# Mixture-of-experts stage: token rows gathered as 128 halves of 2 KB instead of 64 rows of 4 KB

## What is computed

```python
def hier_moe(x, g_ffn, w_group, w_router, w_gate, w_up, w_down):
    h = rmsnorm(x, g_ffn).reshape(b * t, d)                  # d = 1024
    ...                                                      # best of 4 groups, then the best 2 of its 8 experts
    def add_expert(acc, params):
        wg, wu, wd, c = params                               # 1024x512, 1024x512, 512x1024 each
        act = jax.nn.silu(h @ wg) * (h @ wu)
        return acc + (act @ wd) * c[:, None], None
    out, _ = lax.scan(add_expert, jnp.zeros_like(h), (w_gate, w_up, w_down, combine))   # 32 experts
```

## Time and profile before

| | |
|---|---|
| median of 3 runs | 1159.38 us (1159.24 to 1162.21) |
| profiled execution | 1159.31 us, its span 1157.5 us |
| TensorE | 1026.8 us busy, 89% of the span |
| VectorE, ScalarE, GpSimd | 433.2, 243.2, 298.5 us |
| DMA | 304.27 MB, mean 263 GB/s; from slice 25 on about 400 |

### The profile page before, as it was taken

How to read it: one execution, slowest core, us unless ns; L and a number is a source line. 1 busy time by engine, 2 the same in 40 slices (tenths; PEclk the granted TensorE clock), 3 DMA queues, 4 the chain that set the end, 5 groups by cost and what they waited for, 6 DMA issues and landing times. The chain is left out here.

```text
span 1157.5 us, 16104 instructions
## 1 busy us (share of the span) xinstructions
PE 1026.8 (89%) x5989; PEld 574.5 (50%) x5989; DVE 433.2 (37%) x1203; ACT 243.2 (21%) x550; POOL 298.5 (26%) x262
## 2 busy tenths in 40 slices
PE   6999999998999999989999499998777778877786
PEld 3644444446777775323565355454434445444443
DVE  3655888886557555222344211111111111011122
ACT  2122321113444554210043111111110110111011
POOL 1033414533544433002000123222312222221211
PEclk9999999999999999999999699999999999999999
DMA  6331132236756346797482889999999999999993
GB/s 204 93 105 41 52 111 100 83 112 208 230 156 216 112 142 248 256 369 232 192 344 111 331 345 401 401 389 388 403 404 403 400 398 409 402 406 402 405 398 113
DMA packets 82465, 304.27 MB, mean 263 GB/s; under 512 B 23138, under 2 KB 27362, under 8 KB 70226
## 3 DMA queue, kind: packets, MB, share of 16 engines
q1 hardware_dynamic: 64658, 273.47, 61.9%
q0 software_dynamic: 9824, 16.98, 5.2%
q10 hardware_dynamic: 7904, 12.78, 3.0%
HBM read 290.09 MB, written 29.72 MB: 276 GB/s over the span
## 5 line engine op out<-in xcount | busy, mean ns | idle before, releaser
L403 PE MATMUL p_z<-k_w,k_xT 128*128 128x512 f32 (+2 forms) x528 | 208.1, 548 | 0.0
L403 PEld LDWEIGHTS p_z<-k_w,k_xT 128*128 128x128 f32 (+1 forms) x528 | 92.0, 188 | 102.1 <-issue 100.9
L871 PE MATMUL a_G<-k_xT,k_w 128*128 128x260 f32 x512 | 127.6, 394 | 0.0
L2036 DVE TENSOR_TENSOR e_hid<-e_hid,e_G 128x256 f32<-128x256 f32 x32 | 13.5, 421 | 262.4 <-ACT e_hid L1949 262.4
L1954 ACT ACTIVATE e_y<-e_Y,x_share 64x512 f32<-64x512 f32 x64 | 43.7, 683 | 319.7 <-PE e_Y L1839 310.8
L871 PEld LDWEIGHTS a_G<-k_xT,k_w 128*128 128x128 f32 x512 | 93.3, 192 | 26.5 <-issue 13.6
L966 POOL TENSOR_TENSOR k_x<-k_x 128x512 f32<-128x512 f32 x64 | 80.5, 1271 | 89.6 <-DVE k_side L1032 67.2
L2077 POOL DMA_INDIRECT out_y_p<-e_y,x_table x32 | 45.0, 1408 | 215.8 <-ACT e_y L1954 133.3
L156 POOL DMA_INDIRECT k_rows<-token_rows,x_table x32 | 31.3, 978 | 165.9 <-PE e_TX L1819 154.0
L2041 DVE TENSOR_TENSOR e_hid<-e_hid,e_U 128x256 f32<-128x256 f32 x32 | 13.5, 421 | 133.6 <-PE e_U L1825 133.6
L1242 PE MATMUL g_ring<-k_oT,k_w 128*128 128x512 f32 x128 | 60.1, 616 | 0.0
(11 more groups left out here) (354 smaller groups left out, 1468.0 us busy)
## 6 DMA issues: line engine op xcount, KB each, us to landing
k_w<-in_w_in SPq DMA_DIRECT2D x11, 2048.0 KB, 8.2
k_xT<-in_w_down SPq DMA_DIRECT2D x11, 2048.0 KB, 45.2
x_page<-in_w_down SPq DMA_DIRECT2D x10, 2048.0 KB, 44.1
x_w_out<-in_w_down SPq DMA_DIRECT2D x10, 2048.0 KB, 44.5
k_w<-in_w_gate SPq DMA_DIRECT2D x8, 2048.0 KB, 41.9
k_w<-in_w_up SPq DMA_DIRECT2D x8, 2048.0 KB, 45.1
k_oT<-in_w_gate SPq DMA_DIRECT2D x8, 2048.0 KB, 44.3
k_side<-in_w_up SPq DMA_DIRECT2D x8, 2048.0 KB, 44.7
```

The source lines that it names most:

```text
L403: last = nc.tensor.matmul(z[u % 3][0:p, 0:WIDTH[k]], s.xT[:, j, 128 * i:128 * i + p], s.w[:, c % 2, j, 0:WIDTH[k]], start=j == 0, stop=j = ...
L871: last = nc.tensor.matmul(G[u % 2][:, 0:HT], s.w[:, q % 2, j, 128 * c:128 * c + 128], s.xT[:, j, HT * h:HT * h + HT], start=j == 0, stop=j ...
```

## The change

Each token row is gathered as two halves of 512 numbers. Place q's first half lands in partition q, its second in partition 64 + q, so a gather fills 128 partitions with 2 KB each. It has 128 indices (`s.halves`: twice the row number, plus one in the upper 64 partitions). Four transposes of 128 by 128 turn them, and VectorE's copy takes the two halves of each as separate blocks. To have the table in all 128 partitions, `place` now writes both halves of `Rk` at once, and two operations on VectorE make `s.halves` before `s.table`. The output adds still use `s.table` with 64 places.

```diff
+    c[:, C_HALF] = (p >= CAP) - 2.0
...
-    nc.gpsimd.indirect_dma_start(out=s.xg[n], out_offset=None, in_=s.rows[:, :],
+    nc.gpsimd.indirect_dma_start(out=s.xg[n], out_offset=None, in_=s.half_rows[:, :],
                                  in_offset=bass.IndirectOffsetOnAxis(ap=rows, axis=0),
-                                 bounds_check=TOK - 1, oob_is_err=False).then_inc(s.xg_in[n], 16)
+                                 bounds_check=2 * TOK - 1, oob_is_err=False).then_inc(s.xg_in[n], 16)
...
             def place(i):
-                v.tensor_tensor(Rk[0:p, :, 0, :], bcast(iota(CAP)[0:p], 2, 1), bcast(rank, CAP, 2), ALU.is_equal)
+                v.tensor_tensor(Rk[0:p], bcast(bcast(iota(CAP)[0:p], 2, 1), 2, 1), bcast(bcast(rank, 2, 2), CAP, 3), ALU.is_equal)
...
             def share(i):
-                v.tensor_tensor(Rk[0:p, :, 1, :], bcast(iota(CAP)[0:p], 2, 1), bcast(rank, CAP, 2), ALU.is_equal)
...
             dve.wait_ge(tabled, TILES)
-            link(v.tensor_scalar(unfilled, TBt[0:CAP, :], 0.0, NO_ROW, ALU.is_equal, ALU.mult))
-            v.scalar_tensor_tensor(s.table[:, 0:NE], TBt[0:CAP, :], -1.0, unfilled, ALU.add, ALU.add).then_inc(table_ready, 1)
+            v.tensor_scalar(unfilled, TBt, 0.0, NO_ROW, ALU.is_equal, ALU.mult)
+            link(v.tensor_scalar(twice, TBt, 2.0, s.c[:, C_HALF:C_HALF + 1], ALU.mult, ALU.add))
+            v.tensor_tensor(s.halves[:, 0:NE], twice, unfilled, ALU.add).then_inc(table_ready, 1)
+            v.scalar_tensor_tensor(s.table[:, 0:NE], TBt[0:CAP, :], -1.0, unfilled[0:CAP, :], ALU.add, ALU.add)
...
-        TX, AT = ps("TX", [128, KD, CAP]), s.bankO[:, 0:256].rearrange("p (f t) -> p f t", f=2)
+        TX, AT = ps("TX", [128, 4, 2 * CAP]), s.bankO[:, 0:256].rearrange("p (f t) -> p f t", f=2)
...
         def turn_rows(j):
-            for b in range(KD):
-                last = nc.tensor.transpose(TX[:, b, :], xg[j][:, 128 * b:128 * b + 128], s.ident[0:CAP, 0:CAP])
+            for c in range(4):
+                last = nc.tensor.transpose(TX[:, c, :], xg[j][:, 128 * c:128 * c + 128], s.ident[:])
             return last
...
+            def turned_into(j):
+                return v.tensor_tensor(xT[:, j].rearrange("p (h c) q -> p h c q", h=2), TX[:].rearrange("p c (h q) -> p h c q", h=2),
+                                       bcast(s.gffn[:].rearrange("p (h c) -> p h c", h=2), CAP, 3), ALU.mult)
...
             for n in range(2):
-                gather_rows(nc, s, n, s.table[:, n:n + 1])
+                gather_rows(nc, s, n, s.halves[:, n:n + 1])
...
-                    gather_rows(nc, s, e % 2, s.table[:, e + 2:e + 3])
+                    gather_rows(nc, s, e % 2, s.halves[:, e + 2:e + 3])
...
+    s.half_rows = s.rows.rearrange("t (h d) -> (t h) d", h=2)
...
+        s.halves = sb("halves", [128, NBLK], I32)
...
-        s.xg = [s.rowbuf[0:CAP, 2 * n + 2:2 * n + 4, :].rearrange("p a w -> p (a w)") for n in range(2)]
+        s.xg = [s.rowbuf[:, n + 2, :] for n in range(2)]
```

More of the change, by code:

```diff
@@ L45 @@
 C_E, C_ET, C_HM, C_IOTA, C_TOK, C_THR, C_MH, C_PAR = 896, 960, 968, 976, 1040, 1045, 1061, 1069
-C_DH, C_DB, C_SB, C_END = 1070, 1074, 1082, 1086
+C_DH, C_DB, C_SB, C_HALF, C_END = 1070, 1074, 1082, 1086, 1087
 def constants():
@@ L67, in constants @@
     c[:, C_DB:C_SB] = (p[:, None] % 32 // 4) == np.arange(8)
-    c[:, C_SB:C_END] = (p[:, None] % 32 // 8) == np.arange(4)
+    c[:, C_SB:C_HALF] = (p[:, None] % 32 // 8) == np.arange(4)
+    c[:, C_HALF] = (p >= CAP) - 2.0
     return c
@@ L1152, in merge @@
         Lm, Lm2, C = (small[:, 40 + 32 * n:72 + 32 * n] for n in range(3))
-        unfilled, early = small[0:CAP, 232:232 + NE], small[0:CAP, 264:264 + NE]
+        unfilled, early, twice = small[:, 232:232 + NE], small[0:CAP, 264:264 + NE], small[:, 392:392 + NE]
         prank = small[:, 296:296 + 2 * NE].rearrange("p (k e) -> p k e", k=2)
@@ L1780, in experts @@
         sem = lambda n: ctx.enter_context(nc.semaphore("e_" + n))
-        idx = sb("idx", [CAP, 2], I32)
+        idx = sb("idx", [128, 3], I32)
         xg = s.xg
@@ L1795, in experts @@
         eid = spare[:, 180:180 + NX + 1]
-        unfilled, early = spare[0:CAP, 200:200 + NX], spare[0:CAP, 216:216 + NX]
+        unfilled, early, twice = spare[:, 200:200 + NX], spare[0:CAP, 216:216 + NX], spare[:, 232:232 + NX]
         cmp = spare[:, 256:256 + NE * NX].rearrange("p (a b) -> p a b", a=NE)
@@ L1977, in spread @@
                     dve.wait_ge(u_done, e - 1)
-                v.tensor_tensor(xT[:, e % 2], TX[:], bcast(s.gffn[:], CAP, 2), ALU.mult).then_inc(xT_out, 1)
+                turned_into(e % 2).then_inc(xT_out, 1)
             link = Chain(dve, extra_chain)
@@ L2025, in tables_out @@
                 dve.wait_ge(extra_tabled, 1)
-                link(v.tensor_scalar(unfilled, TB[0:CAP, 0:NX], 0.0, NO_ROW, ALU.is_equal, ALU.mult))
-                link(v.scalar_tensor_tensor(s.table[:, NE:NBLK], TB[0:CAP, 0:NX], -1.0, unfilled, ALU.add, ALU.add))
+                link(v.tensor_scalar(unfilled, TB[:, 0:NX], 0.0, NO_ROW, ALU.is_equal, ALU.mult))
+                link(v.tensor_scalar(twice, TB[:, 0:NX], 2.0, s.c[:, C_HALF:C_HALF + 1], ALU.mult, ALU.add))
+                link(v.tensor_tensor(s.halves[:, NE:NBLK], twice, unfilled, ALU.add))
+                link(v.scalar_tensor_tensor(s.table[:, NE:NBLK], TB[0:CAP, 0:NX], -1.0, unfilled[0:CAP, :], ALU.add, ALU.add))
                 link(v.tensor_scalar(early, TB[0:CAP, 0:NX], 1.0 + SEQ, NO_ROW, ALU.is_lt, ALU.mult))
@@ L2057, in step @@
                 dve.wait_ge(x_turned, b + NE + 1)
-                v.tensor_tensor(xT[:, 0], TX[:], bcast(s.gffn[:], CAP, 2), ALU.mult).then_inc(xT_out, 1)
+                turned_into(0).then_inc(xT_out, 1)
                 dve.wait_ge(gated, b + NE + 1)
@@ L2099, in step @@
                 pool.wait_ge(x_turned, b + NE)
-                nc.gpsimd.tensor_copy(idx[:, 0:1], s.table[:, bass.ds(b + NE, 1)]).then_inc(idx_ready, 1)
-                nc.gpsimd.tensor_copy(idx[:, 1:2], s.to_s[:, bass.ds(b + NE, 1)]).then_inc(idx_ready, 1)
-                pool.wait_ge(idx_ready, b * 3 + 2)
+                nc.gpsimd.tensor_copy(idx[:, 0:1], s.halves[:, bass.ds(b + NE, 1)]).then_inc(idx_ready, 1)
+                nc.gpsimd.tensor_copy(idx[0:CAP, 1:2], s.table[:, bass.ds(b + NE, 1)]).then_inc(idx_ready, 1)
+                nc.gpsimd.tensor_copy(idx[0:CAP, 2:3], s.to_s[:, bass.ds(b + NE, 1)]).then_inc(idx_ready, 1)
+                pool.wait_ge(idx_ready, b * 4 + 3)
                 pool.sem_inc(idx_ready, 1)
@@ L2106, in step @@
                 pool.sem_inc(y_passed, 1)
-                add_rows(0, idx[:, 0:1], idx[:, 1:2])
+                add_rows(0, idx[0:CAP, 1:2], idx[0:CAP, 2:3])
                 pool.wait_ge(y_added, b * 32 + NE * 32 + 32)
```

## The result

The changed kernel takes **1139.27 us** (median of 4, 1138.33 to 1140.74) against 1159.31 (median of 4, 1157.98 to 1162.21) before, a ratio of 0.9822 with an interval of 0.9802 to 0.9842. It is faster by 20 us, 1.8%.

A forecast was written before the change was run, and what follows sets the result against it. Weight bytes through the DMA queues were taken to bound the expert stage. From 1159.31 us, relief -15.6, more packets +1.9 and the head +2.9 gave -10.8, so 1148.5 us; range 1143 to 1165, own range 1143 to 1153.

The forecast's parts named there:

- What bounds the kernel: Expert stage, about 670 to 1141 us: weight bytes through the DMA queues set the time, slowed while gathered rows arrive.
- Relief, -15.6: Weight stream: gathers into 128 partitions take the slump away for 29 gathers, 15.6 us saved.
- The price of 0.54 us a gather: Weight stream, 830 to 1130 us: slow weight packets cost 9.1 us over 17 gathers, 0.54 us each.
- More packets, +1.9: Weight stream: 128 halves instead of 64 rows per gather make more packets, 1.9 us added.
- The head, +2.9: Before expert 0: VectorE's added work and a longer first gather delay the stream by 2.9 us, bounds 0.3 and 4.
- The four more turns beside the weight queue: First gather: 8 pieces per engine instead of 4, alternating with weight packets, 2.4 us added, bounds 0 and 2.6.
- VectorE's operations: Head: wider placing of tile 3 and added operations before the stage's last copy, 0.3 us added.
- Turns, nothing: TensorE's transposes of gathered rows: four of 128 columns instead of eight of 64, no change in time.
- The third, shared turns: Rival: added pieces share turns, so the head costs 0.5 us instead of 2.9, total 1146.1 us; chance 0.06.
- The first, half relief: Rival: engines' pieces go to partitions other engines feed, so collisions spread; -7.8 us relief, total 1156.3 us; chance 0.24.
- The second, no relief: Rival: the burst of 32 scattered rows causes the slump, so weights stay slow; total 1164.1 us; chance 0.24.
- The explanation by ports: Gathers in the stream: partitions 0 to 63 reach only 8 of 16 SBUF ports, hence the slump; no separate size.

The follow-up runs named there:

- mirrored against mirrored: Places 32 to 63 of each expert filled from the far end, in the kernel before (1153.92 us) and in the changed kernel (1134.96 us).
- the mirrored kernel: The changed kernel with places 32 to 63 of each expert filled from the far end: 1134.96 us.
- the long list: The kernel before, same 4 KB rows in partitions 0 to 63, with an index list of 128 places, the upper 64 out of bounds: 1154.46 us.
- the two gathers of halves apart: The kernel before with 2 KB halves by two gathers of 64 places, into partitions 0 to 63 and 64 to 127: 1161.14 us.
- the spread: The changed kernel with an expert's filled places spread over the list, rank 8j + g at place 8g + j: 1158.89 us.

## Why the prediction was right or wrong

**What bounds the kernel: right.** The weights' bytes set the time, the slump behind each gather was the loss, and it went where the prediction had placed it: 16.04 us per expert (16.1 forecast), 432 GB/s in the stretch where rows arrive, 26.6 KB per us in the weight queue. What it didn't see is that the engines' unequal loads are a second cost, the same before and after the change (44.8 and 44.2 us on the first engine, by the count above).

**Relief, -15.6: too small.** The last landing came 20.7 us earlier, and the head gave 1.2 of these, so the stream gave 19.5; with even loads, mirrored against mirrored, it is 19.0. The price of 0.54 us a gather for the slow weights was nearly right. From 690 to 1100 us, with 27 gathers, the weight queue moved 25.5 KB per us before and 26.6 after:

```profile
q1 hardware_dynamic: 12487, 156.69, 93.5%
...
q1 hardware_dynamic: 12963, 163.34, 93.6%
```

That is 15.2 us, 0.56 for each, or 16.3 for 29. What the sum left out is the rest. The gathered packets are faster too: for the gathers of experts 15 to 29 queue 0 spent 189 ns a row before and 161 after, which over the 952 rows of 29 gathers is 1.6 us. The prediction had put up to 3.8 us for this into the range, from 225 ns a row in one stretch of 3 us. And in the last 16 us before the landing the engines idled 4.4 us before and 3.0 after, which gives another 1.4. With these the stream comes to 19.3.

**More packets, +1.9: nothing.** The prediction took it that each half is a packet of its own; the counts are equal.

**The head, +2.9: it was -1.2.** The four more turns beside the weight queue rest on the same error and don't exist: the first gather took 8.14 us, not 11 or more. VectorE's operations cost about what was forecast, 0.2 us for 0.3: from the first line of the placing to the last copy it takes 5.53 us instead of 5.32. The profiled execution hides it, since its placing began 0.25 us earlier and the last copy so came at 650.33 instead of 650.37.

```profile
644.80 0.23 DVE L1672 TENSOR_TENSOR g_scp<-g_ring,x_oh 128x64 f32<-128x64 f32 x1 [0.29 <-PE g_ring L1332]
...
650.33 0.19 DVE L1773 COPY x_share<-x_O 128x32 f32<-128x32 f32 x1 [1.13 <-PE x_O L1351]
```

GpSimd holds a gather of 128 places for 1.05 us instead of 0.98, 0.07 where 0.2 had been put. Expert 0's up product starts at 667.28 where it was 668.47, and so the next weight loads go out 1.2 us sooner. One execution of each stands behind this: the mirrored kernel, whose head is the same, started that product at 668.22, so the size of the head's gain is not sure.

**Turns, nothing: right.** Four transposes take 0.59 us instead of 0.64, beside the loads.

The stream's 19.5 and the head's 1.2, less 0.8 us more behind the last landing (17.8 instead of 16.9), are the 19.9 by which the two profiled executions differ; the 19.5 is what this leaves to the stream. So the steps that failed are the added packets and their turns, priced at 1.9 and 2.4 us and nothing in the runs, and the relief, 3.9 too small. Even with every term at its most favourable bound the sum gives 1140.8; no bound allowed that the added pieces make no packets, or that the head gets shorter.

**The rivals.** The third, shared turns, was what happened, and had 0.06; the page of the Trainium skill that it names fits, and I read 41 packets beside 41 in the earlier trace rows as 41 turns without asking what one record holds. But taking out the turns alone gives 1146.1. Of the 6.7 us from there to the measured time the relief has 3.9, the packets 1.9 and the head 1.7, against 0.8 at the end. The first, half relief, had the idea that the explanation below needs, in the wrong kernel: pieces that go to partitions other engines feed. It was asked of the change; by the mapping it holds for the kernel before. The second, no relief, is refuted: by it the burst of scattered rows itself slows the weights, and in the changed kernel the same burst does not.

**The explanation by ports: only half right.** The prediction followed the Trainium skill, "SBUF — State Buffer", section "Door 1: The DMA port swizzle": 64 partitions, 8 of 16 ports. But the long list writes all its rows through the same 8 ports, and its weights are not slowed; the two gathers of halves apart use all 16 ports and slow them. What is shown is the condition: one transfer that reaches over all 128 partitions keeps the rate (four kernels of two lengths of list and two sizes of piece), transfers over 64 lose it. What may lie behind it is who writes through a port. A weight load covers 128 partitions, and by the page's mapping engine 0 alone writes 0 to 3 and 32 to 35; a gather over all 128 would keep to that. A gather over 64 would send two engines to each of the lower ports, and only engine 0 would meet its own. The Trainium skill, "DMA: Bandwidth & Descriptors", section "Back-pressure in remote DMA", says of transfers between cores that a stalled write stalls the engine's other queues too. If that holds here as well, the weights of an engine wait behind a row that meets a busy port. The slump agrees with it, but no run here looks inside an engine, so this last step is argued, not shown. The page's mapping of a transfer to 128 partitions, taken for the gather, would have spoken against the first rival before the change.

## What to carry to other kernels

Beside a full stream of weights, let one transfer of the gather reach over all 128 partitions, as the stream's do, with 128 places or with every other partition; two transfers of 64 neighbouring partitions do not do it. It is not the pieces' size that counts. Then count the rows by engine: where places are filled from the front, some engines always have more, and a fixed permutation of the places can be worth several us or cost 20. When a queue shows the full rate and its last transfer is late, look at the DMA share in the last us before it lands: 0.5 or 0.25 there says what part of the engines everything waits for.

## What was not expected of the hardware

- The same 1040 rows and the same 128 partitions cost 22 us more in two gathers of 64 places than in one of 128 (1161.14 against 1139.27 us).
- Changing nothing but the order of the places within an expert moves the kernel by 24 us: 1134.96 with the mirror, 1158.89 with the spread.
- Two halves of 2 KB from different rows travel as one packet: the change doubles the pieces, and the count of packets stays at 82465.
- 2048 more places out of bounds cost no rate: the queue of the long list moved 107.99 MB where that of the change moved 108.04.
